# Merged rows of a transformer layer reach their transposed layout through VectorE and DMA instead of TensorE

## What is computed

```python
def token_mixing(xn, ...):
    ...                                   # four attention branches o_a, o_b, o_c, o_d from xn @ w_in
    z = xn @ gate_down
    merged = None
    for i, (o, wb) in enumerate(zip((o_a, o_b, o_c, o_d), jnp.split(w_branch, BRANCH_OFFSETS, axis=0))):
        gate = jax.nn.sigmoid(z @ gate_up[i])
        term = gate * (o @ wb)
        merged = term if merged is None else merged + term
    return merged @ w_out

h = h + token_mixing(rmsnorm(h, norm_mix[l]), ...)
h = h + peer_ffn(rmsnorm(h, norm_ffn[l]), ...)   # top-16 of 4096 experts per head, then wmat @ v
```

## Time and profile before

| | us |
|---|---|
| three executions | 1956.44, 1957.56, 1958.32 |
| the profiled execution | 1957.31 |
| its span, from first to last instruction | 1955.5 |
| TensorE busy | 1943.1 |
| VectorE busy | 1244.3 |
| ScalarE busy | 916.4 |
| POOL busy | 28.2 |

### The profile page before, as it was taken

The page is one execution under the profiler, slowest core; times in us unless marked ns, Lnnn a source line. Parts: engine busy times, 40 slices in busy tenths (PEclk is TensorE's granted clock), DMA queues, the critical chain, the costliest instruction groups (busy, mean ns, idle before and its releaser), DMA issues.

```text
span 1955.5 us, 26523 instructions
## 1 busy us (share of the span) xinstructions
PE 1943.1 (99%) x9239; PEld 1604.8 (82%) x9239; DVE 1244.3 (64%) x1844; ACT 916.4 (47%) x1114; POOL 28.2 (1%) x40
## 2 busy tenths in 40 slices
PE   8999999999999999999999999999999999999999
PEld 7788888888888888888888888888887788888887
DVE  6458474584556887655555555788879876444444
ACT  6544345444456655444444454444444454333332
POOL 0010000010000000000000000000000000000000
PEclk9999999999999999999999999999999999999999
DMA  9876656565655665777777776676776678666664
GB/s 327 281 193 186 212 157 171 168 166 168 188 176 173 182 187 173 254 231 214 215 216 222 226 227 222 228 216 214 215 209 192 188 232 277 205 204 204 203 205 140
DMA packets 189959, 404.21 MB, mean 207 GB/s; under 512 B 44864, under 2 KB 118976, under 8 KB 188320
## 3 DMA queue, kind: packets, MB, share of 16 engines
q1 hardware_dynamic: 167856, 360.44, 61.5%
q10 hardware_dynamic: 20112, 25.19, 3.8%
q0 software_dynamic: 1888, 17.17, 2.3%
HBM read 385.96 MB, written 16.78 MB: 206 GB/s over the span
## 4 chain that ended last, share of the span: by engine, by line
PE 97%; DMA 2%; DVE 1%; SPq 0%; ACT 0%; issue 0%; ACTq 0%
PE acc L492 28%; PE acc L494 28%; PE acc L493 28%; PE acc L509 3%; PE acc L511 3%; PE acc L510 3%; DMA w_raw<-in_w_in 2%; PE side L627 1%; PE side L590 1%; PE side L751 1%; PE side L662 0%; DVE w_lo L1213 0%; PE side L560 0%; PE side L710 0%; DMA xt_raw<-in_xt 0%; PE side L638 0%
## 5 line engine op out<-in xcount | busy, mean ns | idle before, releaser
L1213 DVE TENSOR_TENSOR w_lo<-w_raw,w_hi 128x1024 fp32r<-128x1024 f32 (+1 forms) x680 | 825.7, 1216 | 660.3 <-ACT w_hi L883 657.8
L883 ACT ACTIVATE w_hi<-w_raw 128x1024 fp32r<-128x1024 f32 (+1 forms) x680 | 714.6, 1052 | 843.6 <-PE acc L494 776.8
L492 PE MATMUL acc<-w_hi,xt_hi 128*128 128x512 f32 (+1 forms) x1724 | 673.0, 390 | 9.2 <-DVE w_lo L1213 9.2
L494 PE MATMUL acc<-w_hi,xt_lo 128*128 128x512 f32 (+1 forms) x1724 | 667.5, 387 | 0.0
L493 PE MATMUL acc<-w_lo,xt_hi 128*128 128x512 f32 (+1 forms) x1724 | 667.1, 387 | 0.0
L492 PEld LDWEIGHTS acc<-w_hi,xt_hi 128*128 128x128 f32 x1724 | 324.6, 188 | 75.3 <-issue 7.8
L494 PEld LDWEIGHTS acc<-w_hi,xt_lo 128*128 128x128 f32 x1724 | 324.3, 188 | 65.4
L493 PEld LDWEIGHTS acc<-w_lo,xt_hi 128*128 128x128 f32 x1724 | 324.5, 188 | 63.6 <-issue 0.2
L492 PE MATMUL acc<-w_hi,x_hi 128*128 128x512 f32 x640 | 252.4, 394 | 0.0
L494 PE MATMUL acc<-w_hi,x_lo 128*128 128x512 f32 x640 | 249.7, 390 | 0.0
L493 PE MATMUL acc<-w_lo,x_hi 128*128 128x512 f32 x640 | 249.6, 390 | 0.0
(11 more groups left out here) (257 smaller groups left out, 1297.6 us busy)
## 6 DMA issues: line engine op xcount, KB each, us to landing
w_raw<-in_stream SPq DMA_DIRECT2D x504, 512.0 KB, 4.2
w_raw<-in_w_in SPq DMA_DIRECT2D x16, 496.0 KB, 4.0
w_raw<-in_w_in SPq DMA_DIRECT2D x16, 480.0 KB, 3.8
w_raw<-in_w_in SPq DMA_DIRECT2D x16, 464.0 KB, 3.9
w_raw<-in_w_in SPq DMA_DIRECT2D x16, 448.0 KB, 3.8
w_raw<-in_w_in SPq DMA_DIRECT2D x16, 432.0 KB, 3.8
w_raw<-in_w_in SPq DMA_DIRECT2D x16, 416.0 KB, 4.0
w_raw<-in_w_in SPq DMA_DIRECT2D x16, 400.0 KB, 3.8
```

What stands on the lines that cost most here:

```text
L492: pe.matmul(o, xh, wh, start=first and j == 0, stop=False)
L494: mm = pe.matmul(o, xl, wh, start=False, stop=last and j == 1)
L883: nc.scalar.activation(w_hi[:, slot, 0:width], w_raw[:, slot, 0:width], ACT.Copy).then_inc(hi_ready, 1)
L1213: nc.vector.tensor_tensor(w_lo[:, slot, 0:width], w_raw[:, slot, 0:width], w_hi[:, slot, 0:width].bitcast(F32), ALU.subtract).then_inc(lo_ ...
```

## The change

`turn_rows`, `rows_hi` and `rows_lo` go, with their semaphore `xt_turned`. For branch a VectorE writes its sum to a new tile `mix_rows`, laid out in blocks (the other branches add to `rows` as before, in one instruction for both halves). One slot later, 246 + 3n, VectorE transposes the whole 128 x 1024 tile in 32 by 32 blocks into `mix_blk` (`block_mix`). SyncE stores it in four DMAs of 128 KB to DRAM (`mix_store`, behind the loads of chunks 250 + 3n and 251 + 3n, two DMAs each) and loads it back in one of 512 KB into `mix_t` (`mix_load`, behind the load of chunk 253 + 3n). ScalarE makes `xt_hi` from it in slot 252 + 3n (`mix_hi`, two instructions), VectorE `xt_lo` in slot 253 + 3n (`mix_lo`, two instructions). Tiles and scratch are double. SyncE's loop over the stream is written out for chunks 248 to 275, so that these DMAs have their places in it. POOL's load of x no longer waits for `xt_turned`, only for `gate_used`.

```diff
@@ -222,6 +222,10 @@
     tail0 = cursor[0]
+    mix_rows = at("mix_rows", [P, 4, 4, NT, 32], F32, PJ0 + row)
+    mix_blk = [at(f"mix_blk{i}", [P, 4, 256], F32, PJ0 + 4 * i * KB) for i in range(2)]
+    mix_t = [at(f"mix_t{i}", [P, 4, 2, 2, NT, 32], F32, (PJ0 + row + 4 * KB, tail0 + 8 * KB)[i]) for i in range(2)]
+    mix_d = [nc.dram_tensor(f"mix_blocks{i}", (4, 32, 4, 256), F32, kind="Internal").ap() for i in range(2)]
...
@@ -325,7 +329,7 @@
         "stick_loaded", "subkeys_loaded", "iotas_loaded", "stored")
-    xt_hi_done, xt_lo_done, xt_turned = sems("xt_hi_done", "xt_lo_done", "xt_turned")
+    xt_hi_done, xt_lo_done = sems("xt_hi_done", "xt_lo_done")
     squares_done, rstd_ready, half_ready = sems("squares_done", "rstd_ready", "half_ready")
...
@@ -346,6 +350,8 @@
     act_blocked, act_stored, act_moved = sems("act_blocked", "act_stored", "act_moved")
+    mix_blocked, = sems("mix_blocked")
+    mix_stored, mix_moved = sems("mix_stored0", "mix_stored1"), sems("mix_moved0", "mix_moved1")
     row_copied, row_blocked, row_stored, row_moved = sems("row_copied", "row_blocked", "row_stored", "row_moved")
...
@@ -410,10 +416,13 @@
-    XT_TURN, ROW_HI = {}, {}
+    MIX_BLOCK = {mix_end("a", n) + LEAD + 1: n for n in range(GRP)}
+    MIX_STORE = {mix_end("a", n) + LEAD + 5 + i: (n, (2 * i, 2 * i + 1)) for n in range(GRP) for i in range(2)}
+    MIX_LOAD = {mix_end("a", n) + LEAD + 8: n for n in range(GRP)}
+    MIX_HI = {mix_end("a", n) + LEAD + 7: n for n in range(GRP)}
+    ROW_HI = {}
     for n in range(GRP):
         for j in range(2):
-            XT_TURN[mix_end("a", n) + LEAD + 2 + j] = 2 * n + j
             at_slot = {NX2 // 4: CH_WQ + LEAD, GRP - 1: CH_WQ + 11}.get(n, CH_OUT + (n + 1) * CPG + LEAD + 9)
...
@@ -467,10 +476,38 @@
                         load_in(m * RING + c, g, c, m * RING + (c - RING + 1))
-            with sp.Fori(0, (CH_END - CH_MIX) // RING) as g:
-                for c in range(RING):
-                    load(io["stream"][bass.ds(g * RING + c, 1)].rearrange("a p n -> (a p) n"), c, 1024,
-                         g * RING + (CH_MIX + c - RING + 1))
+            def stream(first, last):
+                with sp.Fori((first - CH_MIX) // RING, (last - CH_MIX) // RING) as g:
+                    for c in range(RING):
+                        load(io["stream"][bass.ds(g * RING + c, 1)].rearrange("a p n -> (a p) n"), c, 1024,
+                             g * RING + (CH_MIX + c - RING + 1))
+            def mix_store(n, parts):
+                sp.wait_ge(mix_blocked, n + 1)
+                if n >= 2:
+                    sp.wait_ge(mix_moved[n % 2], 16 * (n // 2))
+                for a in parts:
+                    sp.dma_start(mix_d[n % 2][:, :, a].rearrange("b i x -> i b x"), mix_blk[n % 2][32 * a:32 * a + 32])\
+                        .then_inc(mix_stored[n % 2], 16)
+            def mix_load(n):
+                sp.wait_ge(mix_stored[n % 2], 64 * (n // 2 + 1))
+                if n >= 2:
+                    sp.wait_ge(xt_lo_done, KT + 2 * (n - 1))
+                sp.dma_start(mix_t[n % 2][:].rearrange("p a q k h j -> p (a q k h j)"),
+                             mix_d[n % 2].rearrange("b i a x -> (b i) (a x)")).then_inc(mix_moved[n % 2], 16)
+            first, last = min(MIX_STORE) // RING * RING, -(-(max(MIX_LOAD) + 1) // RING) * RING
+            stream(CH_MIX, first)
+            for s in range(first, last):
+                load(io["stream"][s - CH_MIX], s % RING, 1024, s - RING + 1)
+                if s in MIX_STORE:
+                    mix_store(*MIX_STORE[s])
+                if s in MIX_LOAD:
+                    mix_load(MIX_LOAD[s])
+            stream(last, CH_END)
             for h in range(NT):
...
@@ -696,20 +733,6 @@
                 mm.then_inc(stick_out, 1)
-            def turn_rows(q):
-                pe.wait_ge(gate_used, 3 * GRP + q // 2 + 1)
-                if q < 4:
-                    pe.wait_ge(stick_lo, 2)
-                if q >= 4:
-                    pe.wait_ge(xt_lo_done, KT + q - 3)
-                k = 2 * q
-                for j in range(2):
-                    for h in range(NT):
-                        mm = pe.transpose(side[:, q % 4, j * S + h * P:j * S + (h + 1) * P],
-                                          rows[:, h, (k + j) * P:(k + j + 1) * P], ident[:])
-                mm.then_inc(xt_turned, 1)
...
@@ -782,8 +805,6 @@
                     stick_values(STICK_V.index(s))
-                if s in XT_TURN:
-                    turn_rows(XT_TURN[s])
                 for n in range(4):
...
@@ -1003,11 +1024,14 @@
-            def rows_hi(q):
-                act.wait_ge(xt_turned, q + 1)
-                nc.scalar.activation(flat(xt_hi[:, 2 * q:2 * q + 2, :]), side[:, q % 4, :], ACT.Copy)\
-                    .then_inc(xt_hi_done, 1)
+            def mix_hi(n):
+                act.wait_ge(mix_moved[n % 2], 16 * (n // 2 + 1))
+                for j in range(2):
+                    k = 4 * n + 2 * j
+                    nc.scalar.activation(
+                        xt_hi[:, k:k + 2, :].rearrange("p k (h a j) -> p k h a j", h=NT, a=4),
+                        mix_t[n % 2][:, :, j].rearrange("p a k h j -> p k h a j"), ACT.Copy).then_inc(xt_hi_done, 1)
...
@@ -1159,8 +1183,8 @@
                     gates(s, *GATE_OUT[s])
-                if s - LEAD in XT_TURN:
-                    rows_hi(XT_TURN[s - LEAD])
+                if s in MIX_HI:
+                    mix_hi(MIX_HI[s])
                 for n in range(2):
...
@@ -1431,17 +1455,33 @@
                 else:
-                    for h in range(NT):
-                        dst = rows[:, h, n * 512:(n + 1) * 512]
-                        e = nc.vector.tensor_tensor(dst, dst, gate[:, n % 2, h, :], ALU.add)
+                    if b == "a":
+                        for h in range(NT):
+                            term = rows[:, h, n * 512:(n + 1) * 512].rearrange("p (k b j) -> p k b j", b=4, j=32)
+                            e = nc.vector.tensor_tensor(
+                                mix_rows[:, :, :, h, :].rearrange("p b k j -> p k b j"), term,
+                                gate[:, n % 2, h, :].rearrange("p (k b j) -> p k b j", b=4, j=32), ALU.add)
+                    else:
+                        term = rows[:, :, n * 512:(n + 1) * 512]
+                        e = nc.vector.tensor_tensor(term, term, gate[:, n % 2], ALU.add)
                     e.then_inc(gate_used, 1)
-            def rows_lo(q):
-                dve.wait_ge(xt_hi_done, KT + q + 1)
-                nc.vector.tensor_tensor(flat(xt_lo[:, 2 * q:2 * q + 2, :]), side[:, q % 4, :],
-                                        flat(xt_hi[:, 2 * q:2 * q + 2, :]).bitcast(F32), ALU.subtract)\
-                    .then_inc(xt_lo_done, 1)
+            def block_mix(n):
+                dve.wait_ge(gate_used, 3 * GRP + n + 1)
+                if n >= 2:
+                    dve.wait_ge(mix_stored[n % 2], 64 * (n // 2))
+                nc.vector.transpose(mix_blk[n % 2][:].rearrange("p b x -> p (b x)"),
+                                    mix_rows[:].rearrange("p b k h j -> p (b k h j)")).then_inc(mix_blocked, 1)
+            def mix_lo(n):
+                for j in range(2):
+                    k = 4 * n + 2 * j
+                    dve.wait_ge(xt_hi_done, KT + 2 * n + j + 1)
+                    out, hi = (x[:, k:k + 2, :].rearrange("p k (h a j) -> p k h a j", h=NT, a=4) for x in (xt_lo, xt_hi))
+                    nc.vector.tensor_tensor(out, mix_t[n % 2][:, :, j].rearrange("p a k h j -> p k h a j"),
+                                            hi.bitcast(F32), ALU.subtract).then_inc(xt_lo_done, 1)
...
@@ -1711,8 +1751,10 @@
                     merge(s, *MIX_OUT[s])
-                if s - LEAD - 1 in XT_TURN:
-                    rows_lo(XT_TURN[s - LEAD - 1])
+                if s in MIX_BLOCK:
+                    block_mix(MIX_BLOCK[s])
+                if s - 1 in MIX_HI:
+                    mix_lo(MIX_HI[s - 1])
                 if s - 1 in ROW_HI:
...
@@ -1805,7 +1847,6 @@
             pool.dma_start(iotas[:], io["iotas"]).then_inc(iotas_loaded, 16)
-            pool.wait_ge(xt_turned, KT // 2)
             pool.dma_start(rows[:], io["x"]).then_inc(x_loaded, 16)
...
```

## The result

The changed kernel takes 1961.19 us in the median of 22 executions (1956.82 to 1963.49), the kernel before 1957.33 us in as many (1956.01 to 1958.64). The ratio is 1.0019 with a 95% interval of 1.0013 to 1.0026: it is slower by 3.9 us, where 2.6 us of gain was forecast, and 0.4 us above the upper end of the range. The profiled execution took 1960.20 us, 2.89 more than the profiled one before. Two executions measured later, one of the kernel before at 3283 us and one of an experiment at 3104 us, both with a mean granted clock under 0.6, are left out of every comparison.

A forecast was written before the change was run, and what follows sets the result against it. TensorE, busy 99% of the span, was taken as the bound. 1957.31 - 7.1 (transposes) + 4.5 (wait near chunk 271) = 1954.7 us, against the median 1955.0; range 1950.4 to 1960.8, leaving out the worst of C.

The forecast's parts named there:

- The gain of 7.1 us: Merge stage, TensorE: 64 transposes in 16 calls of `turn_rows` disappear, all on the path, 7.1 us less.
- The place of the loss: Start of w_out: TensorE waits once for w_lo near chunk 271, some 20 us behind the last merge.
- the term for the wait: Near chunk 271: w_lo ready at 20.7 to 21.3, wanted at 16.3; wait of 4.4 to 5 us, 4.5 taken.
- rival C: Merge stage: slower, as the landing of `mix_load` becomes the bound; 1962.5 us, mild half 1960.8; chance 0.2.
- C's chain: Merge stage, one VectorE transpose to that two groups on: 11.3 + landing, against 16.66 us; decides from landing 5.4.
- The third term: Under the load of x: it lands at 15.8 us, `mix_load(6)` after it, at 17.3 to 17.9.
- stalls nobody at first: Merge stage: VectorE's added work makes nobody wait at first, as w_lo has 5.8 us of lead.
- 3.2 us of lead: Merge stage: VectorE's last w_lo of a group comes 2.6 us late, leaving 3.2 us before TensorE wants it.
- from level to 0.2 us short: Merge stage: with the new transpose VectorE is full, from level to 0.2 us short in each group.
- B: Rival: everything is covered, TensorE has no wait; 1950.5 us, up to 1953.6; chance 0.28.
- The advice beside it: Skill page cited for C: use TensorE for a 128 x 128 transpose where PSUM will do; the old way is cheaper.
- The rule of turns by packet: Load of x: a DMA engine takes a packet in turn from each queue with work, so 1 KB stores fare worse.

The follow-up runs named there:

- paced_x: Changed kernel with x loaded in eight DMAs of 512 KB, one for each three chunks from chunk 271 on: 1952.59 us, ratio 0.9975.
- paced_early: Changed kernel with the edits of paced_x and early_load together, measured twice: 1950.55 us, ratio 0.9966, and 1951.21 us, ratio 0.9968.
- late_x: Changed kernel, but POOL's load of x waits until VectorE has made the last xt_lo: 1955.62 us, ratio 0.9990.
- early_load: Changed kernel, but SyncE issues `mix_load(n)` before the two stores of group n+1: 1958.34 us, ratio 1.0005.
- small_x: Changed kernel, but x is loaded at the same place in eight DMAs of 512 KB issued one behind the other: 1957.73 us, ratio 1.0002.
- mid_x: Changed kernel, but POOL's load of x waits until `mix_load(6)` has landed: 1960.49 us, ratio 1.0014.
- paced_two: paced_x with a second VectorE transpose in each group, into a tile that nobody reads: 1953.01 us, ratio 0.9975.
- keep_busy: Changed kernel with 26 matmuls that nobody reads in front of chunk 271: 1959.24 us, ratio 1.0008.
- burst_272: Changed kernel with x in one DMA of 4 MB, issued behind TensorE's chunk 271: 1954.48 us, ratio 0.9989.

## Why the prediction was right and wrong

**The gain of 7.1 us: right.** The three traces without a wait, of paced_x and paced_early, have 7.2 us less, and a group takes 8.32 us as the prediction's 36 matmuls do.

**The place of the loss: right.** One wait for w_lo at chunk 271, 14 us behind the end of the last merge (the sum had 15), released by a chain through `mix_load(6)` and ScalarE, caused by the load of x; late_x and paced_x take it away.

**Its size: wrong, and this is the step that failed.** The sum was 1957.31 - 7.1 + 4.5 = 1954.7; the profiled execution took 1960.20. Of the 5.5 us between them 2.4 are in the term for the wait and 2.9 in a term that the sum put at nothing, the clock; 0.2 is left over.

The wait: "It waits 4.4 to 5, I take 4.5", and it was 6.9. Two terms were too small. VectorE's merge of group 7 ended at 2.6, not at 1.1, and the load of x followed it. The first multiply of group 3 was already 1.7 us behind the 8.32 us beat of the groups, that of group 7 was 3.0 behind; in between ScalarE waited 0.43, 0.58 and 1.37 us for `mix_load`. The landing that I took as 4.4 to 5.4 us is 5.7 in the median, above the 5.4 from which rival C was to decide. C's chain was thus at work, if mildly; early_load took 1.5 us of lateness away. The burst took 14.3 us, not 13.8. The third term held: `mix_load(6)` landed 2.0 us behind the burst's end, where the sum had 1.5 to 2.1, and w_lo was ready 3.4 us after that, as forecast. early_load adds that the issue time of the load hardly matters while the burst runs.

**The term that was missing: the clock.** The prediction gives a stop of TensorE no cost beyond its length. The kernel before has no stop of over 1.5 us behind its start, and its rows show a clock of 1.00 throughout. The stop of 6.9 us brought 2.9 us on top. Without it the profiled execution would have been level with the kernel before. With the wait as forecast, 4.5 us, the clock would have fallen too, to go by small_x, which stopped for 4.7 us and had 8 matmuls at half clock, 1.6 us. The sum would have been near -1.0, not -2.6.

**VectorE "stalls nobody at first", with 3.2 us of lead: wrong in who waits, without harm here.** The short lead is at the first multiply of a group, which the next branch product waits for. In the changed kernel's trace it costs under 0.1 us, in mid_x 0.8; paced_two shows that it is what ends first. That VectorE is full "from level to 0.2 us short" was close for the last groups, 8.25 of 8.32; the first four, with no or the first `mix_lo`, still had 1.05 to 1.65 us idle each, where the prediction looked for under 0.3.

**Rivals.** B (all covered) was wrong for this kernel, and is what paced_early reaches. C named the right magnitude, 1960.8 to 1962.5, for a reason that contributed little. The advice beside it, to leave 128 x 128 transposes to TensorE where PSUM will do (the Trainium skill, VectorE: DVE Perf Modes, Rules for kernel authors), fits the time of the change as it was made, and not the way of transposing: paced_early transposes in the same new way and is 0.3% faster than the kernel before. The rule of turns by packet, which the prediction drew on (the Trainium skill, DMA: Bandwidth & Descriptors, Queues, rings and completion order), fits small_x alone: with packets of 3.7 KB from POOL and 2.2 from SyncE the two got 842 and 720, near one for one; with large ones they got 127 and 557. Whether a packet of the profile is what the page means by one is not shown.

## What to carry to other kernels

Taking work from the bounding engine gives its full time only if nothing else moves: ask of each wait that is removed together with it what it had kept apart; here it had kept a 4 MB load 16 us away from the new transfers. A large load that is not urgent belongs in pieces, each with its own due time; pieces alone, issued at once (small_x), took away only part of the wait, and so did a later burst (late_x). When a forecast contains a stop of TensorE of a few microseconds, add what the clock takes afterwards, and check every wait of the bounding engine on the engine that gets the new work, not only the one with the most traffic.

## What was not expected of the hardware

In the four traces with a stop of 4.7 to 7.5 us the granted clock fell to 0.50 between 2.8 and 5.5 us after TensorE had stopped (in small_x 0.8 us after it had gone on), and 8 to 13 matmuls ran at half clock. Stops of 2.5 to 2.9 us had both outcomes: none low in the trace of late_x, 8 matmuls in keep_busy and in burst_272, where the low stretch began 1.3 to 1.5 us after work had resumed. The same kernel can do either: late_x has a mean clock of 1.000 in three of eleven executions, burst_272 in five of twelve, keep_busy in nine of eleven.

One burst of 4 MB beside a stream of 512 KB loads took between 13.8 and 16.7 us. What sets the length is open: the changed kernel and keep_busy issue it at the same place behind the same loads, and it took 14.3 and 16.7. It held back nearly everything issued after it until it had landed: the weight loads issued in its first 6.5 us took 14 to 17 us in the changed kernel, early_load and keep_busy, against 4.2 in the median of a whole execution.
